# Mamba-2 and attention decoder step on one core: chunk work put ahead of weight conversions, and the step sizes' series moved to GpSimd

## The chip, the cores and the metric

The kernel runs on one core of a Trainium2 chip. The core has five engines: TensorE (PE, matmuls into the PSUM banks), VectorE (DVE), ScalarE (ACT), GpSimd (POOL) and SyncE (SP, which only issues DMAs here). They run on their own and meet at semaphores. The metric is the device time of one launch in microseconds, the median of several runs; lower is better.

## What is computed

One inference step of a two-layer decoder for 256 prompt tokens and 8 sample tokens (N = 264 columns, the model width is 1024). Everything is float32. Layer 0 is half-SwiGLU, Mamba-2 mixer, half-SwiGLU, gated per-layer embedding; layer 1 has sliding-window attention in the mixer's place. The part that the change touches most is the mixer:

```python
def mamba2_mixer(u, w_in, conv_w, conv_b, dt_bias, a_log, d_skip, norm_g, w_out, ssm0, conv0):
    z, xbc, dt_raw = jnp.split(u @ w_in, [D_INNER, D_INNER + CONV_DIM], axis=-1)
    conv = conv_b + sum(xbc_full[:, k:k + t_len] * conv_w[k] for k in range(CONV_W))
    xs, bm, cm = jnp.split(jax.nn.silu(conv), [D_INNER, D_INNER + SSM_GROUPS * D_STATE], axis=-1)
    dt = jax.nn.softplus(dt_raw + dt_bias)          # the step sizes, 32 heads
    a = -jnp.exp(a_log)
    y, h_last = ssd_scan(xs, dt, a, bm, cm, ssm0)   # chunks of 128 tokens, 8 groups of 4 heads
    gated = (y + d_skip[:, None] * xs) * jax.nn.silu(z)
    gg = gated.reshape(bsz, t_len, 8, 256)
    gg = gg * lax.rsqrt(jnp.mean(gg * gg, axis=-1, keepdims=True) + EPS)
    return (gg * norm_g) @ w_out, h_last, ...
```

The softplus is computed as max(t,0) + 2·artanh(q) with q = e/(2+e), e = exp(-|t|), and artanh(q) by its series in q², summed from the last term inwards. In each chunk the scan needs decays between positions (an exponential), the products inside the chunk, a sum over the chunk for the state, and for the second chunk what the first one's state adds.

## The kernel before

**Units.** Every weight matrix is cut into units of 128×1024. A unit is loaded by SyncE into one of four ring slots (`raw`); ScalarE rounds it to a high part (`whi`, L976) and VectorE subtracts to get the low part (`wlo`, L1388). These two are called the conversion here. TensorE then does 24 matmuls for a unit, three for each 128 rows (L435 to L437: high with high, high weights with low data, low weights with high data). In each engine's program `ahead(stage, i, s)` in slot `s` converts the unit that is four places further on, so that unit `s+4` is converted in slot `s`; ScalarE's half waits until TensorE has used unit `s`.

**The stage "sin".** It is the input projection of the mixer, 49 units in 49 slots, in an order written by hand (`SIN`): slot 0 is the step sizes' unit, slots 1 to 3 are `z` tiles, then come eight groups of four `conv` tiles, with further `z` tiles between them. For each slot every engine has its own list of what it does, in program order:
- TensorE: `sin_unit(s)`, then the small matmuls. A unit may only start when an older bank has been taken: unit 9 and later ones wait for the take of unit s-2.
- VectorE: the take (L1435, bank times `rstd`), three taps of the convolution for the previous slot's tile (L1636), `ahead`, and then whatever else stands in the slot.
- ScalarE: `ahead`, the convolution's last tap (`tap_last`, L1133), silu of the previous tile (L1139 or L1144), and whatever else stands in the slot. It loads a table when it changes between exponential, silu and root.
- GpSimd: a copy of each `conv` tile's tail (L2016), small products for the sample tokens, the sum of pairs of squares (L2046) and some DMAs.

**Step sizes.** VectorE takes the unit of slot 0 and starts (`dt_take`, `dt_start` in slot 1), runs the series in slots 2 and 3 (`dt_series`, L1604) and closes it (`dt_end`, L1617 to L1620). In slot 4 ScalarE's `gather_steps` makes eight copies into `dd` (L1186, L1187, tile `small`), and TensorE turns them in slot 7 (`pre_tokens`, L840). Ahead of its slots GpSimd prepares constants (L1994 to L2009, `pre_const`).

**Chunks.** For group g the slots C = `CHUNK_AT[g]` (14, 17, 21, 25, 30, 35, 41, 46), C+1 and C+2 hold: on TensorE `chunk_in` (L744 to L757: transposes and the decay's exponents, for chunk 0 in slot C, for chunk 1 in C+1) and `chunk_out` (L770, L775; chunk 0 in C+1, chunk 1 in C+2); on VectorE `chunk_in` (three operations that read the bank, L1710 to L1712), `decay` (L1732, it waits for ScalarE's exponential L1167), `carry` (L1719; L1723 to L1727) and in C+3 `finish`; on ScalarE `select` (L1158) and the exponential in `decay_exp`. TensorE's L744 for the next chunk waits for VectorE's L1712, its L770 for L1732, its L784 (`add_inter`) for L1723.

**Gate and sums.** In the slots `GATE_AT` VectorE multiplies by the silu of z (`gate`, L1752), ScalarE squares two tiles (L1230), GpSimd adds the two (L2046), and one slot later TensorE sums over the partitions (`norm_sums`, L822). After the eighth group come a root and a reciprocal, and then the output projection.

**Attention.** Eight pairs of heads go through scores (L561 to L565), maxima, exponentials (L1305), probabilities, `transposes` (L575), and `weighted_sum` (L589 to L593), with the rotary products `turn` (L547, L548). VectorE's `low_o(t)` (L1906) empties the bank that `weighted_sum(t+1)` writes.

## Time and profile before

| | before |
|---|---|
| median of 3 runs | 1243.44 us (1242.85 to 1243.95) |
| the profiled execution's own time | 1243.75 us |
| its span, from first to last instruction | 1241.9 us |
| mean granted TensorE clock | 0.994 of full speed |
| busy share of the span | TensorE 97%, VectorE 71%, ScalarE 56%, GpSimd 18% |
| stage "sin" | 211 to 445 us of the span |

The profile is of one execution. A busy share is an average over stages with different limits. The time outside the span, 1.85 us, belongs to the launch. Times in the text are microseconds from the start of the span.

### The profile page before, as it was taken

How to read it: one execution, taken by the hardware profiler on the slowest of the kernel's cores; microseconds unless marked ns; L12 is line 12 of the kernel's file. 1: busy time of each engine (PE TensorE's matmuls, PEld its weight loads, DVE VectorE, ACT ScalarE, POOL GpSimd, SP SyncE). 2: the span in 40 equal slices, each digit the busy share in tenths (PEclk: the TensorE clock that was granted, in tenths of full speed). 3: DMA queues.
4: the chain of work that ended last, by engine and by line, in shares of the span. 5: the costliest groups of instructions: out<-in, count | busy, mean ns of one | idle time of the engine just before them, and what ended most of it. 6: DMA issues, size and time to landing. Idle time of an engine off the chain costs nothing.

```text
span 1241.9 us, 26744 instructions
## 1 busy us (share of the span) xinstructions
PE 1207.8 (97%) x9887; PEld 1172.6 (94%) x9887; DVE 882.6 (71%) x1405; ACT 691.3 (56%) x1098; POOL 225.5 (18%) x332
## 2 busy tenths in 40 slices
PE   7999999889999999999999999999999999999998
PEld 7999999878888899999999989999998899999998
DVE  6667646978888876767744988788369758776447
ACT  6444436666566546555545774555357656445335
POOL 0000003212121110122244333332015310000001
PEclk9999999989999999999999999999999999999999
DMA  7665555645444445858786666766753146555552
GB/s 281 233 201 183 185 173 172 217 142 174 141 151 152 140 147 179 325 186 285 227 322 222 228 238 216 260 198 223 253 162 103 60 136 196 176 186 182 175 185 87
DMA packets 61424, 239.08 MB, mean 193 GB/s; under 512 B 7080, under 2 KB 8272, under 8 KB 56976
## 3 DMA queue, kind: packets, MB, share of 16 engines
q1 hardware_dynamic: 55008, 197.01, 47.7%
q0 software_dynamic: 6064, 40.66, 9.3%
q8 instruction: 42, 0.69, 0.2%
q10 hardware_dynamic: 288, 0.54, 0.1%
q14 instruction: 22, 0.18, 0.0%
HBM read 226.87 MB, written 13.39 MB: 193 GB/s over the span
## 4 chain that ended last, share of the span: by engine, by line
PE 79%; DVE 12%; ACT 5%; issue 4%; DMA 0%; DVEq 0%; SPq 0%; POOL 0%; ACTq 0%
PE bank L435 24%; PE bank L436 24%; PE bank L437 24%; DVE wlo L1388 3%; ACT whi L976 2%; DVE xl L1407 1%; DVE xact L1636 1%; PE bank L467 1%; PE bank L775 1%; PE bank L770 1%; DVE x L1418 1%; DVE rstd L1429 1%; DVE gu L1435 1%; PE bank L811 0%; ACT L1167 0%
## 5 line engine op out<-in xcount | busy, mean ns | idle before, releaser
L1388 DVE TENSOR_TENSOR wlo<-raw,whi 128x1024 fp32r<-128x1024 f32 x369 | 458.6, 1247 | 259.2 <-ACT whi L976 258.1
L435 PE MATMUL bank<-xh,whi 128*128 128x264 f32 x2024 | 583.6, 288 | 14.7 <-DVE xl L1407 9.8
L436 PE MATMUL bank<-xl,whi 128*128 128x264 f32 x2024 | 575.7, 284 | 0.0
L437 PE MATMUL bank<-xh,wlo 128*128 128x264 f32 x2024 | 575.3, 284 | 0.0
L976 ACT ACTIVATE whi<-raw 128x1024 fp32r<-128x1024 f32 x369 | 387.6, 1054 | 271.7 <-PE bank L437 262.4
L435 PEld LDWEIGHTS bank<-xh,whi 128*128 128x128 f32 x2024 | 383.4, 189 | 20.2 <-DVE wlo L1388 11.6
L436 PEld LDWEIGHTS bank<-xl,whi 128*128 128x128 f32 x2024 | 383.7, 190 | 0.9
L437 PEld LDWEIGHTS bank<-xh,wlo 128*128 128x128 f32 x2024 | 381.8, 189 | 0.0
L435 PE MATMUL bank<-hh,whi 128*128 (+1 forms) x896 | 255.9, 286 | 1.7 <-DVE xact L1503 0.9
L437 PE MATMUL bank<-hh,wlo 128*128 (+1 forms) x896 | 255.0, 285 | 0.0
L436 PE MATMUL bank<-hl,whi 128*128 (+1 forms) x896 | 254.4, 284 | 0.0
L435 PEld LDWEIGHTS bank<-hh,whi 128*128 128x128 f32 x896 | 168.6, 188 | 3.4 <-DVE xact L1503 1.1
L436 PEld LDWEIGHTS bank<-hl,whi 128*128 128x128 f32 x896 | 169.1, 189 | 0.1
L437 PEld LDWEIGHTS bank<-hh,wlo 128*128 128x128 f32 x896 | 168.6, 188 | 0.0
L1043 ACT ACTIVATE hh<-gu 128x264 fp32r<-128x264 f32 (+1 forms) x88 | 37.4, 425 | 164.0 <-DVE gu L1447 164.0
L1980 POOL TENSOR_TENSOR sq<-sq 128x264 f32<-128x264 f32 x42 | 34.0, 809 | 419.2 <-ACT sq L1014 414.8
L1435 DVE TENSOR_TENSOR gu<-bank,rstd 128x264 f32<-128x264 f32 x192 | 82.1, 429 | 19.2 <-PE bank L437 17.0
L1452 DVE TENSOR_TENSOR hl<-gu,hh 128x264 f32 (+1 forms) x88 | 42.4, 482 | 28.9 <-ACT hh L1043 28.9
L2115 POOL TENSOR_TENSOR xact<-xact,da_bc 128x512 f32<-128x512 f32 x32 | 38.9, 1217 | 101.8 <-PE bank L437 101.8
L1636 DVE SCALAR_TENSOR_TENSOR xact<-under,vs,xact 128x256 f32<-128x256 f32 x96 | 46.6, 485 | 3.2 <-ACT xact L1133 0.9
L1447 DVE TENSOR_TENSOR gu<-gu 128x264 f32<-128x264 f32 x88 | 44.9, 510 | 0.1
L2120 POOL TENSOR_TENSOR xact<-xact 128x512 f32<-128x512 f32 x20 | 29.6, 1481 | 60.6 <-PE bank L437 60.6
(309 smaller groups left out, 1002.9 us busy)
## 6 DMA issues: line engine op xcount, KB each, us to landing
raw<-weights SPq DMA_DIRECT2D x369, 512.0 KB, 3.5
under<-ssm POOLq DMA_DIRECT2D x8, 1024.0 KB, 5.1
xact<-ssm POOLq DMA_DIRECT2D x8, 1024.0 KB, 7.3
out_ssm_s<-xact POOLq DMA_DIRECT2D x8, 1024.0 KB, 5.3
xact<-dtx_rows POOLq DMA_DIRECT2D x5, 1024.0 KB, 11.0
zs<-dtx_rows POOLq DMA_DIRECT2D x2, 1024.0 KB, 13.6
x<-xT SPq DMA_DIRECT2D x2, 528.0 KB, 5.5
xact<-stat_rows POOLq DMA_DIRECT2D x2, 528.0 KB, 6.5
```

What stands on the lines that cost most here:

```text
L435: pe.matmul(out, whi[:, w, c], rh, start=start, stop=False)
L436: pe.matmul(out, whi[:, w, c], rl, start=False, stop=False)
L437: return pe.matmul(out, wlo[:, w, c], rh, start=False, stop=stop)
L976: act.activation(whi[:, s, :], raw[:, s, :], ACT.Copy).then_inc(hi_ready, 1)
L1043: act.activation(dst, gu[:, 2 * p + 1, :], ACT.Copy).then_inc(hh_ready, 1)
L1388: dve.tensor_tensor(wlo[:, s, :], raw[:, s, :], whi[:, s, :].bitcast(F32), ALU.subtract).then_inc(lo_ready, 1)
L1435: dve.tensor_tensor(dst, src[:, 0:N], rstd[:, :], ALU.mult).then_inc(a_free, 1)
L1447: dve.tensor_tensor(gu[:, 2 * p + 1, :], gu[:, 2 * p, :], gu[:, 2 * p + 1, :], ALU.mult).then_inc(h_ready, 1)
L1452: dve.tensor_tensor(one(hl), gu[:, 2 * p + 1, :], one(hh).bitcast(F32), ALU.subtract).then_inc(hl_ready, 1)
L1636: dve.scalar_tensor_tensor(out=out, in0=xr[:, k:k + T], scalar=vs[:, V_CW + CT * k + c:V_CW + CT * k + c + 1], in1=out, op0=ALU.mult, op1= ...
L1980: pool.tensor_tensor(sq3[:, 0, :], sq3[:, 0, :], sq3[:, m, :], ALU.add).then_inc(sq_pair, 1)
L2115: pool.tensor_tensor(by_head(part), by_head(part), da_bc[:, 2 * k:2 * k + 2, 4 * q:4 * q + 4].unsqueeze(3).to_broadcast([P, 2, 4, 64]), AL ...
```

## The change

On VectorE the chunk work, the carries and the gate of a slot now stand in front of the slot's conversion (`ahead`) in all slots that hold chunk work, with the gate behind the carries; the first chunk's part is moved one slot forward, to slot 13. On ScalarE the first exponential of a group stands ahead of the gate's square, the very first one right behind the exponentials of slot 12, and `gather_steps` stands behind `tap_last`. The series has one term less and runs on GpSimd, which also makes half of the eight copies. The last group's two squares are summed by TensorE without GpSimd. In attention `transposes(4)` goes ahead of `turn(7)`, and `low_o(3)` ahead of a conversion.

```diff
-DT_STEPS = 18
+DT_STEPS = 9
@@ TensorE
             def norm_sums(g):
-                pe.wait_ge(gated_pair, g + 1)
+                if g < G - 1:
+                    pe.wait_ge(gated_pair, g + 1)
+                else:
+                    pe.wait_ge(gated_sq, G)
...
-                pe.matmul(rows, ones[:, 0:32], gsq[:, 0, :], start=True, stop=True).then_inc(gated_sum, 1)
+                tiles = 1 if g < G - 1 else 2
+                for k in range(tiles):
+                    mm = pe.matmul(rows, ones[:, 0:32], gsq[:, k, :], start=k == 0, stop=k == tiles - 1)
+                mm.then_inc(gated_sum, 1)
             def pre_tokens():
                 pe.wait_ge(dt_a_step, 3)
+                pe.wait_ge(dt_ready, 2)
@@ TensorE, attention
             scores(5)
+            transposes(4)
             turn(7)
-            transposes(4)
@@ ScalarE
             def gather_steps():
-                act.wait_ge(dt_d_step, DT_STEPS)
+                act.wait_ge(dt_ready, 1)
                 for q in range(4):
-                    act.activation(dd[0:32, c], xact[r, 8, 0:66], ACT.Copy)
                     ins = act.activation(dd[32:64, c], xact[r, 14, 0:66], ACT.Copy)
@@ ScalarE, slots
+                if kind == "conv":
+                    tap_last(s_, i)
                 if s_ == 4:
                     gather_steps()
-                if kind == "conv":
-                    tap_last(s_, i)
...
                     ins.then_inc(pre_a, 1)
+                    decay_exp(0)
+                if s_ in CHUNK_AT[1:]:
+                    decay_exp(2 * CHUNK_AT.index(s_))
                 if s_ in GATE_AT:
...
-                if s_ in CHUNK_AT:
-                    decay_exp(2 * CHUNK_AT.index(s_))
@@ VectorE
-                dt_step(dve.tensor_scalar(a_, s2_, 1.0 / 17, None, ALU.mult))
+                dt_step(dve.tensor_scalar(a_, s2_, 1.0 / 15, None, ALU.mult))
+                dt_step(dve.tensor_scalar(avec[:, :], avec[:, :], -1.0, None, ALU.mult))
@@ VectorE, slots
-                if 0 < s_ < len(SIN):
-                    ahead("sin", 0, s_)
                 if s_ == 1:
                     dt_start()
-                if s_ == 2:
-                    dt_series((15, 13, 11, 9))
-                if s_ == 3:
-                    dt_series((7, 5, 3))
-                    dt_end()
+                chunks = s_ == CHUNK_AT[0] - 1 or s_ in CHUNK_AT[1:] or s_ - 1 in CHUNK_AT or s_ - 2 in CHUNK_AT
+                if 0 < s_ < len(SIN) and not chunks:
+                    ahead("sin", 0, s_)
...
-                if s_ in GATE_AT:
-                    gate(GATE_AT.index(s_))
...
-                    if s_ == CHUNK_AT[g]:
+                    if s_ == (CHUNK_AT[g] if g > 0 else CHUNK_AT[0] - 1):
                         chunk_in(2 * g)
                         decay(2 * g)
...
+                if s_ in GATE_AT:
+                    gate(GATE_AT.index(s_))
+                if s_ < len(SIN) and chunks:
+                    ahead("sin", 0, s_)
@@ VectorE, attention
             maxima(5)
+            low_o(3)
             ahead("q", 0, 7)
             rope_sin(7)
             rope_add(7)
-            low_o(3)
@@ GpSimd, behind the constants
+            t_, q_, m_, s2_, a_ = (xact[:, 8 + k, 0:66] for k in (0, 4, 2, 5, 6))
+            pool.wait_ge(dt_d_step, DT_STEPS)
+            for k in (13, 11, 9, 7, 5, 3):
+                link(pool, pool_step, steps, pool.tensor_scalar(a_, a_, 1.0 / k, None, ALU.add))
+                link(pool, pool_step, steps, pool.tensor_tensor(a_, a_, s2_, ALU.mult))
+            link(pool, pool_step, steps, pool.tensor_scalar(a_, a_, 1.0, 2.0, ALU.add, ALU.mult))
+            link(pool, pool_step, steps, pool.tensor_tensor(a_, a_, q_, ALU.mult))
+            pool.tensor_tensor(a_, a_, m_, ALU.add).then_inc(dt_ready, 1)
+            pool.wait_ge(dt_ready, 1)
+            link(pool, pool_step, steps, pool.tensor_scalar(t_, a_, avec[:, :], None, ALU.mult))
+            for q in range(4):
+                r, c = slice(32 * q, 32 * q + 32), slice(66 * q, 66 * q + 66)
+                ins = pool.tensor_copy(dd[0:32, c], xact[r, 8, 0:66])
+                link(pool, pool_step, steps, ins) if q < 3 else ins.then_inc(dt_ready, 1)
+            pool.wait_ge(dt_ready, 2)
@@ GpSimd, slots
-                if s_ in NORM_AT:
+                if s_ in NORM_AT[:G - 1]:
                     pair_squares(NORM_AT.index(s_))
```

`link` lets the engine wait for the operation that it has just issued.

## Rows read from the trace of the kernel before

**Rows 1.** The page, busy time of each engine in the span.

```profile
PE 1207.8 (97%) x9887; PEld 1172.6 (94%) x9887; DVE 882.6 (71%) x1405; ACT 691.3 (56%) x1098; POOL 225.5 (18%) x332
```

**Rows 2.** TensorE's waits, 205 to 445 us: total, times, longest.

```profile
PE bank L744 <- DVE sq L1712: 4.9, 3, 4.2
PE bank L770 <- DVE sq L1732: 3.2, 5, 1.3
PE bank L435 <- DVE under L1435: 2.8, 1, 2.8
...
PE bank L822 <- POOL gsq L2046: 0.7, 1, 0.7
PE bank L784 <- DVE under L1723: 0.7, 1, 0.7
```

**Rows 3.** Windows: busy time and instructions of each engine, granted clock, DMA.

```profile
100.00:200.00 100.00, 100.00 (x826) 100.00 (x825) 54.44 (x66) 41.49 (x50) 0.00 (x0) 1.00 0.56 179
...
237.90:241.30 3.40, 3.40 (x18) 3.40 (x17) 3.33 (x6) 1.77 (x4) 0.67 (x2) 0.50 0.81 272
...
265.20:272.00 6.80, 5.88 (x25) 4.72 (x26) 5.15 (x11) 5.50 (x9) 1.13 (x1) 0.50 0.49 162
```

**Rows 4.** Timeline of VectorE, step sizes: start, us, instruction, idle before.

```profile
218.97 1.38 DVE L1388 TENSOR_TENSOR wlo<-raw,whi 128x1024 fp32r<-128x1024 f32 x1
...
223.43 1.01 DVE L1604 SCALAR_TENSOR_TENSOR xact<-xact 128x66 f32<-128x66 f32 x4
...
230.53 1.53 DVE L1636 SCALAR_TENSOR_TENSOR xact<-under,vs,xact 128x256 f32<-128x256 f32 x3 [0.89 <-ACT xact L1133]
231.97 1.22 DVE L1388 TENSOR_TENSOR wlo<-raw,whi 128x1024 fp32r<-128x1024 f32 x1
...
236.03 0.42 DVE L1435 TENSOR_TENSOR under<-bank,rstd 128x264 f32<-128x264 f32 x1
```

**Rows 5.** Timeline of GpSimd, 211 to 262 us.

```profile
213.29 0.63 POOL L1995 TENSOR_TENSOR gu<-gu,vs 128x256 f32<-128x256 f32 x1
214.00 0.63 POOL L1997 TENSOR_TENSOR gu<-zs,vs 128x256 f32<-128x256 f32 x1
...
228.31 1.04 POOL L2016 COPY tailraw<-under 128x11 f32<-128x11 f32 x1 [6.75 <-DVE under L1435]
229.71 0.19 POOL L2016 COPY tailraw<-under 128x11 f32<-128x11 f32 x1 [0.35 <-DVE under L1435]
233.60 0.39 POOL L2016 COPY tailraw<-under 128x11 f32<-128x11 f32 x1 [3.70 <-DVE under L1435]
```

**Rows 6.** Timeline of ScalarE, 225 to 235 us.

```profile
227.74 0.26 ACT L1186 ACTIVATE small<-xact 32x66 f32<-32x66 f32 x1 [3.95 <-DVE xact L1620]
```

**Rows 7.** Timeline of VectorE, first chunk.

```profile
260.68 1.23 DVE L1388 TENSOR_TENSOR wlo<-raw,whi 128x1024 fp32r<-128x1024 f32 x1 [1.62 <-ACT whi L976]
...
264.98 0.42 DVE L1710 COPY under<-bank 128x256 f32<-128x256 f32 x1
```

**Rows 8.** Timeline of ScalarE, first chunk.

```profile
259.30 0.26 ACT L1223 ACTIVATE dt_d<-bank 64x128 f32<-64x128 f32 x1
...
264.57 1.28 ACT L1167 ACT_TABLE_LOAD   x1
```

**Rows 9.** Timeline of TensorE, first chunk.

```profile
266.12 0.80 PE L744 MATMUL bank<-xact 128*128 128x128 f32 x2 [4.19 <-DVE sq L1712]
...
275.15 0.33 PE L770 MATMUL bank<-sq 128*64 128x128 f32 x2
```

**Rows 10.** VectorE's waits, 205 to 445 us.

```profile
DVE sq L1732 <- ACT sq L1167: 7.2, 7, 1.9
```

**Rows 11.** Timelines of GpSimd and TensorE, sum of the first group.

```profile
294.99 0.76 POOL L2046 TENSOR_TENSOR gsq<-gsq 128x264 f32<-128x264 f32 x1 [5.99 <-ACT gsq L1230]
...
296.32 0.63 PE L822 MATMUL bank<-gsq,cs 128*32 128x264 f32 x2
```

**Rows 12.** Timeline of TensorE, attention.

```profile
975.35 0.44 PE L589 MATMUL bank<-under,xact 128*64 128x128 f32 x4 [1.01 <-DVE hl L1906]
```

More of the change, by code:

```diff
@@ L239, in trunk_kernel @@
         dt_d_step = sem("dt_d_step")
+        dt_ready = sem("dt_ready")
         dt_a_step = sem("dt_a_step")
@@ L1599, in dt_take @@
                 dt_step(dve.tensor_scalar(m_, t_, 0.0, None, ALU.max))
-            def dt_series(ks):
-                for k in ks:
-                    dt_step(dve.scalar_tensor_tensor(out=a_, in0=a_, scalar=1.0 / k, in1=s2_, op0=ALU.add, op1=ALU.mult))
             def dt_start():
@@ L1612, in dt_start @@
                 dt_step(dve.tensor_tensor(s2_, q_, q_, ALU.mult))
-                dt_step(dve.tensor_scalar(a_, s2_, 1.0 / 17, None, ALU.mult))
-            def dt_end():
-                dt_step(dve.scalar_tensor_tensor(out=a_, in0=a_, scalar=1.0, in1=q_, op0=ALU.add, op1=ALU.mult))
-                dt_step(dve.scalar_tensor_tensor(out=a_, in0=a_, scalar=2.0, in1=m_, op0=ALU.mult, op1=ALU.add))
-                link(dve, dve_step, steps, dve.tensor_scalar(avec[:, :], avec[:, :], -1.0, None, ALU.mult))
-                dt_step(dve.tensor_scalar(t_, a_, avec[:, :], None, ALU.mult))
+                dt_step(dve.tensor_scalar(a_, s2_, 1.0 / 15, None, ALU.mult))
+                dt_step(dve.tensor_scalar(avec[:, :], avec[:, :], -1.0, None, ALU.mult))
                 assert n_dt[0] == DT_STEPS
```

## The prediction

> **What bounds the kernel now.** I read the page first, then the waits, the windows and the timelines of the one stage that the edits touch. TensorE is busy for 97% of the span [rows 1], so only the holes in its row can be won. The stage "sin" (the units of the mixer's input projection with the chunked state sums between them) runs from 211 to 445 us of the span. TensorE's waits there add up to 12.9 us, and they name their releasers [rows 2]: one wait of 2.8 us on a take (L1435, the copy of a finished bank to SBUF), 4.9 us on the end of `chunk_in` (L1712), of which 4.2 is one wait, 3.2 us in five waits on `decay` (L1732), and 0.7 us each at L784 and L822. Both long waits are followed by a stretch in which the granted clock is at its lower level, 1.2 GHz [rows 3]. In the first, 3.4 us long, 18 matmuls are issued; at full clock 826 are issued in 100 us, 0.121 us apart, so that 18 need 2.2 us: 1.2 us lost. In the second, 6.8 us, I estimate 2.4 us lost. The two sites therefore cost 2.8+1.2 and 4.2+2.4 us, 10.6 together; that is what the change plays for.
>
> **Site 1: the step sizes.** Before, seven series steps (four of them 1.01 us), two closing ones, a negation and a product (0.9 us) stand between VectorE's conversions [rows 4], and at the first `conv` slot ScalarE waits 3.9 us for them, makes eight copies of 0.27 us, and only then does its `tap_last` (L1133) [rows 6]. VectorE's taps, 0.89 us late for that, start at 230.53 [rows 4], its conversion for unit 9 ends at 231.97+1.22 = 233.20, and the take of unit 7, which TensorE's unit 9 waits for, comes at 236.03; TensorE restarts at 236.60.
>
> After, VectorE is rid of ten small operations (0.25 us each, 2.5 us) and the series is 20 GpSimd operations: six pairs, three closing ones, the product, four copies. Each waits for the one before. A free GpSimd chain of 256 elements goes from start to start in 0.71 us (213.29 to 214.00, 0.63 of it the operation), an 11 element copy takes 0.19 [rows 5]; in between, 66 elements take 0.32 and 0.40 with the link. The 15 operations up to `dt_ready` 1 would then need 6.0 us. But a copy that needs 0.19 took 1.04 under a conversion of VectorE, and 0.39 between two taps: it came out when VectorE's operation ended [rows 5]. So I lay the chain against VectorE's schedule. `dt_start` (now with the negation, 1.9 us) stands ahead of the conversion for unit 5; it ends at about 221.0, and GpSimd's constants end about then too. From there VectorE runs take and conversion in turn (1.65 us), and I count two GpSimd operations for each pair, one held by the conversion and one started in the take: eight operations by 227.6. Three taps let one through each (229.2). Then four more in 1.6 us, because VectorE has stopped: operation 15 ends at 230.8.
>
> VectorE stops because ScalarE now stands in `gather_steps` until `dt_ready` 1. Behind it are a z silu (0.3), the conversions for unit 9 and all later taps. ScalarE: 230.8+0.1+4×0.27+0.3+1.05 = 233.3, VectorE's half 1.25 more: unit 9 is converted at 234.6, against 233.20. VectorE works without a pause in this stretch, so all behind it is 1.4 later: the take of unit 7 at 237.5, unit 9 at 238.0. TensorE also loses 0.9 at unit 5 (its conversion ends at 222.3, where it ended at 218.97+1.38 = 220.35) and 1.7 at `pre_tokens`, which waits for GpSimd's copies (232.8). These two lie before the wait for unit 9 and only shorten it. If the shorter holes leave the clock full, the 1.4 us are paid back by the 1.2 us of the low clock: site 1 is worth 0. Below: a chain that is held once by each of seven VectorE operations and needs 0.83 us elsewhere (the price of 256 elements) ends near 235.7: 5 us lost. Above: a chain that nothing holds ends at 227.0, and all 4.0 us are won. I take 0, as the held copies are the nearest rows.
>
> The Trainium skill (GPSIMD Engine Reference, Performance versus the Vector engine) speaks against the move: a two-input operation takes about twice VectorE's time. With VectorE's 0.23 us for 66 elements the operations would take 0.46, and site 1 would be 1 to 2 us worse than by my interpolation; no GpSimd operation of this size is in the trace.
>
> **Site 2: the first chunk.** TensorE stood at L744 until 266.12, since VectorE did `chunk_in(0)` at 264.98 to 266.06: behind a conversion for which it had waited 1.62 us, taps and another conversion. ScalarE was late for that conversion because of its exponentials with a table load of 1.28, and it loaded the table again at 264.57 [rows 7, 8]. After, chunk 0 follows the taps of slot 13: VectorE 259.1+0.2 (`pre_decode`), `chunk_in` to 260.4; ScalarE goes on from 259.30+0.26 = 259.56 with select 0.39 and the exponential 0.60 without a load, and `decay(0)` ends at 261.3. TensorE arrives at L744 at 266.12-4.19 = 261.9: no wait. What is late next is chunk 1. ScalarE's conversions of slots 13 and 14 are 1 us later, it must load the silu table, wait for VectorE's last tap (264.8), convert (266.5), do the taps of slot 15 after its take (266.6), select, load and exponential: 269.5. TensorE's `decode_rows(0)` waits for that exponential; it is reached at 267.5 and ends at 270.7, where `chunk_out(1)` starts, against 275.15 [rows 9]: 4.5 us won of 6.6.
>
> This is not kept whole. The gate now stands behind the carries and ahead of the conversion. VectorE loses its cover for the wait on ScalarE's exponential (idle 0.4 to 1.9 us before `decay`, 7.2 us in seven waits [rows 10]): before, the conversion filled part of it, and its 1.2 us now come after. Two such delays put `gate(0)` at 291.2 to 291.9; the square ends at 292.6, GpSimd's pair sum (0.76) is held by the conversion that now follows the gate, and TensorE's sum L822 starts at 293.7, against 296.32 [rows 11]. So 2.6 us of the 4.5 are left, and TensorE has a new wait there.
>
> **The other chunks.** TensorE's 3.2 us on `decay`, 0.7 at L744 (without the long one) and 0.7 at L784. L744 goes, since `chunk_in` is 1.2 us earlier. The first `decay` of a group waits for ScalarE, not for VectorE, and gains nothing except in slots 30 and 46, where the exponential now stands ahead of the square (0.65): 1.3 and 0.7 us are won there. The second `decay` comes 1 us earlier, but the sum L822 behind it later. L784 goes: its carry stood behind conversion and gate. At L822 the last pair sum (0.75) goes, a second matmul pair (0.45) comes: 0.3. Sum of what can be won 3.9; with bounds of 0 (every wait replaced) and 4.5 I take 2.5. A conversion that is 3 us later costs nothing itself: four units of 2.9 us lie between it and its use.
>
> **Attention.** TensorE waits 1.0 us for `low_o(3)`, until 975.35 [rows 12]. Moved ahead of a conversion (1.2) and three small rope operations it ends 2 us earlier, and the transposes of pair 4 no longer stand behind 1 us of `turn(7)`: 0.8 won, between 0 (the exponentials were last) and 1.5.
>
> **Sum.** 0 + 2.6 + 2.5 + 0.8 = 5.9 us off the profiled execution's 1243.75 (1241.9 of it span) is 1237.85; the median of the runs is 0.3 below that execution, so 1237.5.
>
> **Rivals.** (a) The series hides: TensorE never waits for GpSimd, and site 2 keeps all. 4.0+6.6+3.9+0.8 = 15.3: 1228.1. For it: the stretches in which GpSimd was idle (6.7 us after 221.57); against: ScalarE's queue. (b) Slower: the chain on GpSimd is late, and all conversions wait behind `gather_steps`. Each us by which operation 15 ends after 229.4 costs one us. It eats the other gains from 235.4 on, 0.97 us per operation, and from 238 the kernel is over 0.2% slower: 1246. Here a GpSimd operation that has started must also hold VectorE. The rows show that only as 1.38 for a conversion instead of 1.21 [rows 4]. The Trainium skill (SBUF — State Buffer, SBUF: two separate sides) calls the shared port pair an exclusive lock for the whole instruction in both directions. By that, the 11 operations up to VectorE's halt would put up to 11×0.32 = 3.5 us on VectorE as well; the 0.17 of the row does not bear that out. (c) The waits only change their names: `decay` still ends last on ScalarE's exponential, L822 waits for the gate, site 1 is lost by 1.5: 1241 to 1245, say 1243.
>
> **Chances.** Forecast (gains of 3 to 10 us) 0.60; (a) 0.12; (b) 0.12; (c) 0.16. The forecast's own range is 1233.5 to 1240.5. The range with no more than 2 in 10 left out reaches from 1231, between forecast and (a), to 1243.5, into (b) and (c). A measurement here can tell about 0.2%, 2.5 us. Faster: 0.56+0.12+0.04 = 0.72; same: 0.04+0.04+0.10 = 0.18; slower 0.10.
>
> **What would show it.** Site 1: ScalarE's wait ahead of its first copy to `small`, now released by GpSimd; conversion 9 near 234.6; GpSimd operations of 0.3 us where VectorE rests and longer where it converts. Site 2: L744 without a wait, TensorE waiting about 2 us for the second exponential, no low clock near 265. Later: L822 waiting for POOL, L784 gone. Wrong it would be if operation 15 ended well before 229 or after 233, or if the low clock came back behind new holes (1 to 2.5 us each).

## The result, and the profile after

The changed kernel takes 1245.96 us (median of 20 runs, 1244.64 to 1248.15), the kernel before 1244.07 (20 runs, 1242.55 to 1245.7). The ratio is 1.0015, with a 95% interval of 1.0009 to 1.0021: 1.9 us slower, where 6 us faster was forecast. That lies inside the 0.2% taken as no change, and outside the forecast range. One execution of all that follow (in experiment 2) took 1305.03 us at a mean granted clock of 0.85; it is in no median and no ratio here.

The profiled execution took 1247.58 us (span 1245.7), 1.6 above its median, so part of its 3.8 us over the span of before isn't the change's. Its mean granted clock is 0.993; 15 of the 20 runs have 0.994 or more. Where the time arises can be read by setting the same events side by side. First the lines of TensorE's waits from 205 to 445 us, as in [rows 2]:

```profile
PE bank L828 <- POOL gsq L2057: 5.6, 7, 1.4
PE bank L848 <- POOL small L2020: 2.3, 1, 2.3
PE bank L797 <- ACT sq L1175: 2.3, 1, 2.3
PE bank L436 <- DVE under L1443: 1.8, 1, 1.8
PE bank L436 <- DVE wlo L1396: 1.4, 2, 0.8
PE bank L771 <- DVE sq L1729: 1.1, 2, 0.6
```

The waits at L744, L784 and most of those at L770 are gone (the lines are L745, L785 and L771 now), as the change intended. In their place stand seven waits at L828, the squares' sum (L822 before), and one at L848, the transposes of the step sizes. The total is 14.5 us, against 12.9 in [rows 2].

The same events of TensorE in its timeline, first of the kernel after:

```profile
265.45 0.38 PE L745 MATMUL bank<-xact 128*128 128x128 f32 x2
...
272.99 1.07 PE L797 MATMUL bank<-under,dact 128*32 128x256 f32 x16 [2.25 <-ACT sq L1175]
273.99 0.33 PE L771 MATMUL bank<-sq 128*64 128x128 f32 x2
...
295.86 0.63 PE L828 MATMUL bank<-gsq,cs 128*32 128x264 f32 x2 [0.63 <-POOL gsq L2057]
...
426.77 0.63 PE L828 MATMUL bank<-gsq,cs 128*32 128x264 f32 x2 [0.88 <-POOL gsq L2057]
...
441.93 1.08 PE L828 MATMUL bank<-gsq,cs 128*32 128x264 f32 x4
...
719.41 0.59 PE L436 MATMUL bank<-xh,whi 128*128 128x264 f32 x1 [1.20 <-DVE xl L1415]
```

and three of before that [rows 9, 11] don't hold:

```profile
427.07 0.63 PE L822 MATMUL bank<-gsq,cs 128*32 128x264 f32 x2
...
440.80 0.63 PE L822 MATMUL bank<-gsq,cs 128*32 128x264 f32 x2 [0.71 <-POOL gsq L2046]
...
717.34 0.39 PE L435 MATMUL bank<-xh,whi 128*128 128x264 f32 x1 [1.20 <-DVE xl L1407]
```

| event | before | after | lag |
|---|---|---|---|
| GpSimd's constants [rows 5] | 213.29 | 214.64 | +1.35 |
| take of unit 7 [rows 4] | 236.03 | 239.72 | +3.69 |
| L744, first chunk [rows 9] | 266.12 | 265.45 | -0.67 |
| L770, second chunk [rows 9] | 275.15 | 273.99 | -1.16 |
| sum of group 0 [rows 11] | 296.32 | 295.86 | -0.46 |
| sum of the sixth group | 427.07 | 426.77 | -0.30 |
| last sum | 440.80 | 441.93 | +1.13 |
| second hole of a unit at 717 | 717.34 | 719.41 | +2.07 |
| end of the span | 1241.9 | 1245.7 | +3.8 |

The first 1.35 us arise ahead of everything that was changed and the comparison starts from there. The step sizes lose 2.3 us, the first chunk wins 4.9, the first sum takes 0.7 back, and the groups between 296 and 427 us win nothing. Up to the last sum 1.4 are then lost, and they are a stretch at the lower clock (below): TensorE's L814 at 428.25 is 0.30 ahead of its row of before (L813, 428.55), and 24 matmuls later L771 at 433.09 is 1.23 behind (L770, 431.86), with no wait between. Another 1.0 is there by 491 (the next row that both have starts at 491.38 for 489.25): the last sum has four matmuls and holds the next unit for 1.00 us instead of 0.56, and 0.3 is a wait for a conversion. The order alone (experiment 1) loses the same 1.0 there, so it belongs to the change. Behind 717 two stretches at the lower clock take 1.4 and 1.5 us (719 us, and the second half of the one at 982), and attention wins 1.1 between them.

The granted clock in the profile's windows of the kernel after (columns as in [rows 3]):

```profile
241.20:244.60 3.40, 3.40 (x18) 3.40 (x17) 3.33 (x7) 1.38 (x3) 1.05 (x2) 0.50 0.74 246
428.90:432.30 3.40, 3.40 (x18) 3.40 (x17) 2.90 (x5) 2.13 (x3) 0.00 (x0) 0.51 0.08 12
719.10:722.50 3.40, 3.09 (x14) 3.09 (x15) 2.77 (x5) 3.38 (x5) 1.40 (x2) 0.50 0.19 39
981.90:988.70 6.80, 6.80 (x49) 5.93 (x50) 2.39 (x10) 2.61 (x10) 3.52 (x8) 0.50 0.06 20
```

The stretch at 1.2 GHz near 265 is gone. The one behind unit 9 has stayed, and a new one stands at 429, behind the 0.88 us wait at L828. Another stands at 719, behind holes of 0.96 and 1.20 us that the kernel before has too (its row 717.34); in the kernel before the granted clock is 1.00 in the whole window from 715 to 721. The one at 982 is there before the change as well, but half as long (3.4 us).

### The step sizes

GpSimd's timeline of the kernel after, and under it VectorE's and ScalarE's:

```profile
222.66 1.37 POOL L2011 TENSOR_SCALAR xact<-xact 128x66 f32<-128x66 f32 x1 [0.66 <-DVE avec L1617]
224.12 1.31 POOL L2012 TENSOR_TENSOR xact<-xact 128x66 f32<-128x66 f32 x1
225.51 1.44 POOL L2011 TENSOR_SCALAR xact<-xact 128x66 f32<-128x66 f32 x1
227.03 1.34 POOL L2012 TENSOR_TENSOR xact<-xact 128x66 f32<-128x66 f32 x1
228.46 0.38 POOL L2011 TENSOR_SCALAR xact<-xact 128x66 f32<-128x66 f32 x1
...
232.82 0.32 POOL L2015 TENSOR_TENSOR xact<-xact 128x66 f32<-128x66 f32 x1
```

```profile
222.54 1.23 DVE L1396 TENSOR_TENSOR wlo<-raw,whi 128x1024 fp32r<-128x1024 f32 x1
223.68 0.42 DVE L1443 TENSOR_TENSOR zs<-bank,rstd 128x264 f32<-128x264 f32 x1
224.02 1.21 DVE L1396 TENSOR_TENSOR wlo<-raw,whi 128x1024 fp32r<-128x1024 f32 x1
...
235.67 1.23 DVE L1396 TENSOR_TENSOR wlo<-raw,whi 128x1024 fp32r<-128x1024 f32 x1 [5.62 <-ACT whi L984]
```

```profile
233.18 1.06 ACT L1194 ACTIVATE small<-xact 32x66 f32<-32x66 f32 x4 [5.49 <-POOL xact L2015]
```

The first four operations of the series come out when a conversion of VectorE ends (223.77, and the next ones), and each has missed the gap behind it: the conversion is over at 223.77, GpSimd's operation at 224.03, the next conversion starts at 224.02, GpSimd's next operation at 224.12. So one operation passes in 1.45 us. Where VectorE makes taps or rests, the other eleven take 4.7 us, 0.43 each; four of them start inside the three taps (228.45 to 230.05) and take 0.33 to 0.44, so no hold shows there. Meanwhile ScalarE stands for 5.5 us and VectorE for 5.6.

### A sum of squares

Group 0 in the kernel after, VectorE, ScalarE and GpSimd:

```profile
292.25 0.42 DVE L1720 TENSOR_TENSOR under<-bank,tok 128x256 f32<-128x256 f32 x1
...
293.37 0.70 DVE L1749 TENSOR_TENSOR zs<-zs,xact 128x528 f32<-128x528 f32 x1
293.99 1.22 DVE L1396 TENSOR_TENSOR wlo<-raw,whi 128x1024 fp32r<-128x1024 f32 x1
```

```profile
294.10 0.65 ACT L1240 ACTIVATE gsq<-zs 128x528 f32<-128x528 f32 x1 [0.84 <-DVE zs L1749]
```

```profile
294.83 0.98 POOL L2057 TENSOR_TENSOR gsq<-gsq 128x264 f32<-128x264 f32 x1 [6.84 <-ACT gsq L1240]
```

The gate (L1749) stands behind the three operations of the carry, the square behind the gate, the pair sum behind the square and under a conversion (0.98 us for 0.76 in [rows 11]), and TensorE, which has the sum in its program one slot behind the gate, waits for it until 295.86. Six other groups do the same.

### The profile page after: what moved, and what is told of

Its sections match the earlier page's. It is cut to its first block, busy times and chain, and to the rows that moved or that the text cites. A ratio compares the mean times of both kernels' runs of the same rounds, so it can differ in the third digit from the quotient of the medians.

```text
span 1245.7 us, 26753 instructions
## 1 busy us (share of the span) xinstructions
PE 1209.1 (97%) x9889; PEld 1174.3 (94%) x9889; DVE 879.6 (71%) x1395; ACT 688.8 (55%) x1094; POOL 234.1 (19%) x351
## 4 chain that ended last, share of the span: by engine, by line
PE 75%; DVE 13%; ACT 6%; issue 4%; POOL 1%; DMA 1%; DVEq 0%; SPq 0%; ACTq 0%; POOLq 0%
PE bank L436 23%; PE bank L437 23%; PE bank L438 23%; DVE wlo L1396 4%; ACT whi L984 2%; DVE xact L1633 1%; DVE xl L1415 1%; PE bank L468 1%; ACT L1175 1%; DVE x L1426 1%; DVE rstd L1437 1%; DVE gu L1443 1%; DMA x<-xT 1%; DMA xact<-stat_rows 1%; POOL gsq L2057 0%
```

## The experiments

All ratios are to the kernel before, measured in turn with it on the same chip, with 95% intervals; microseconds won or lost are worked out from the ratio and its 1244. A lag is the start of an event less the start of the same event in the kernel before.

**1. The change in three parts.** The first has only the hunks of the series and the copies, the second only those of the order, the early first chunk, the exponentials and the last sum, the third only the two moves in attention. Together they are the changed kernel.

The series alone:

> The kernel before with one part of the change alone: the step sizes' series and half of the copies on GpSimd. Theory (what the trace of the changed kernel shows): four operations of the series are each held to the end of a VectorE conversion, the last value comes at about 231.8 us instead of the forecast 230.8, unit 9 starts 2.3 us later than before, the low clock stays: 2.0 to 2.5 us slower than before. Rival (the forecast): 0, the shorter holes leave the clock full. Second rival: the loss of the first stretch is made up by the wait of the first chunk (4.2 us, it is VectorE's), which then would shrink only if VectorE weren't late as well: under 1 us slower.

1246.15 us, 1.0021 (1.0011 to 1.0030): 2.6 us slower. The forecast of 0 falls. Its TensorE waits 2.6 us at the transposes, 0.3 at unit 9 and 1.4 in two smaller ones; the stretch at 1.2 GHz follows the transposes here.

The order alone:

> The kernel before with the chunk work, carries and gate in front of the conversions on VectorE, the exponentials in front of the squares on ScalarE, and the last group's sum on TensorE; series and attention as before. Theory: the first chunk's wait and its low clock go (3.5 to 4.5 us won), the other chunks win nothing, as each wait for a decay or a carry comes back as a wait for the pair sum on GpSimd (0.6 to 1.3 us at each of seven sums), and the end of the stage loses 1 to 2 us: 1 to 3 us faster than before. Rival (the forecast): 5.1 us faster. Rival: no gain at all, if the low clock of the first chunk comes back at a later hole.

1242.07 us, 0.9992 (0.9983 to 1.0001): 1.0 us faster, where the prediction had 5.1, at the lower end of the 1 to 3 of the text above. Its waits in TensorE:

```profile
PE bank L827 <- POOL gsq L2056: 5.4, 7, 1.4
PE bank L435 <- DVE under L1442: 2.9, 1, 2.9
PE bank L796 <- ACT sq L1173: 2.3, 1, 2.3
```

The seven waits at the sums are there without the series on GpSimd. The first and the last sum:

```profile
293.54 0.63 PE L827 MATMUL bank<-gsq,cs 128*32 128x264 f32 x2 [0.39 <-POOL gsq L2056]
...
438.08 1.08 PE L827 MATMUL bank<-gsq,cs 128*32 128x264 f32 x4
```

Against 296.32 and 440.80 before, the lag is -2.78 at the first sum and -2.72 at the last, and -1.71 at 489: from the first sum on the order wins nothing and then loses the 1.0 us named above. There is no stretch at 1.2 GHz at 429 in this execution, though the wait ahead of there is nearly the same (0.90 us at the sixth sum for 0.88).

Attention alone:

> The kernel before with only the two moves in attention. Forecast: 0.8 us faster (0 to 1.5). Theory from the changed kernel's trace: the weighted sum of pair 4 starts 1.1 us earlier there, but a stretch at the lower clock behind it is twice as long (6.8 us for 3.4) and takes 1 to 1.8 us: 0 to 0.5 us slower. If that stretch has nothing to do with the moves, 0.8 to 1.1 faster.

1242.83 us, 0.9994 (0.9982 to 1.0006): 0.7 us faster, as the prediction had it (0.8), though the interval reaches from 2.2 faster to 0.7 slower and so holds the 0 to 0.5 slower of the text above too. The three parts add up to 0.9 us slower, each with about 1.1 us either way; the whole change measured 1.9.

**2. Two cures for the sums.** Both start from the order alone. One leaves the gate where it was ahead of the change's move, in front of the chunk work:

```diff
+                if s_ in GATE_AT:
+                    gate(GATE_AT.index(s_))
                 for g in range(G):
                     if s_ == CHUNK_AT[g] + 3:
                         finish(g)
...
-                if s_ in GATE_AT:
-                    gate(GATE_AT.index(s_))
                 if s_ < len(SIN) and chunks:
```

> As the run with the order of the chunk work alone, but the gate stands ahead of the chunk work and the carries, as in the kernel before. Theory: the 5.4 us at TensorE's seven sums come from the gate behind the decays and carries and from GpSimd's pair sum held by the conversion behind it; with the gate first the square is done before it: these waits fall to 1 to 2 us, 0.5 to 1 us come back at decays and carries (0.7 us of gate ahead of them): 2.5 to 4 us faster than with the order alone. Rival: ScalarE's square stands behind its exponential and is as late as before, then nothing changes.

1237.21 us, 0.9944 (0.9931 to 0.9957): 7.0 us faster than before, 6.0 faster than the order alone, more than the 2.5 to 4 expected. TensorE's waits:

```profile
PE bank L435 <- DVE under L1442: 2.9, 1, 2.9
PE bank L796 <- ACT sq L1173: 2.3, 1, 2.3
PE bank L770 <- DVE sq L1739: 1.1, 2, 0.6
PE bank L827 <- ACT gsq L1239: 0.8, 1, 0.8
```

5.4 us in seven waits have become 0.8 in one; those at the decays (L770) are what they were with the order alone, so the gate in front of them costs nothing there. A wait of 0.7 us at L744 for a silu (`ACT xact L1145`) is new. So the waits give 3.9 of the 6.0 us; the rest I can't assign (the two intervals together allow about 2 either way). The first and the last sum:

```profile
292.05 0.63 PE L827 MATMUL bank<-gsq,cs 128*32 128x264 f32 x2
...
433.25 1.08 PE L827 MATMUL bank<-gsq,cs 128*32 128x264 f32 x4 [0.82 <-ACT gsq L1239]
```

The lag goes from -4.27 to -7.55: with the gate first the same order wins 3.3 us between the two sums, 2.1 of them left at 489. In the first group VectorE and GpSimd:

```profile
288.89 0.70 DVE L1759 TENSOR_TENSOR zs<-zs,xact 128x528 f32<-128x528 f32 x1
...
290.63 1.73 DVE L1395 TENSOR_TENSOR wlo<-raw,whi 128x1024 fp32r<-128x1024 f32 x1
```

```profile
290.52 0.75 POOL L2056 TENSOR_TENSOR gsq<-gsq 128x264 f32<-128x264 f32 x1 [5.91 <-ACT gsq L1239]
```

The pair sum is finished at 291.27, before TensorE comes to its sum at 292.05.

The other cure leaves the gate behind the carries and asks for the sum later:

```diff
-NORM_AT = [t_ + 1 for t_ in GATE_AT]
+NORM_AT = [t_ + (2 if g_ in (0, 1, 2, 3, 4, 5) else 1) for g_, t_ in enumerate(GATE_AT)]
```

> As the run with the order of the chunk work alone, but TensorE's and GpSimd's part of the first six groups' sums one slot later. Theory: the waits at the first six sums (about 5 us) are there because the sum comes one slot behind a gate that now stands behind the carries; a slot later (2.9 us) they have gone: 3 to 5 us faster than the run with the order alone. Rival: the waits only move on, to the next decay, as ScalarE's exponential and the conversions set the pace: within 1 us of it.

1238.28 us, 0.9955 (0.9941 to 0.9968): 5.6 us faster than before, 4.6 faster than the order alone. The waits for the pair sum fall to 0.4 us; the decays have 0.5 for 1.1, so nothing moved on to them. A wait of 0.9 us at one sum has no releaser in the profile.

**3. How much of it is GpSimd's.** TensorE sums both tiles of every group, and GpSimd adds none; the gate stays behind the carries.

```diff
-                if g < G - 1:
-                    pe.wait_ge(gated_pair, g + 1)
-                else:
-                    pe.wait_ge(gated_sq, G)
+                pe.wait_ge(gated_sq, g + 1)
...
-                tiles = 1 if g < G - 1 else 2
+                tiles = 2
...
-                if s_ in NORM_AT[:G - 1]:
-                    pair_squares(NORM_AT.index(s_))
```

> As the run with the order of the chunk work alone (gate behind the carries), but TensorE sums both tiles in all groups, GpSimd adds no pair. It splits the 5.4 us at the sums: the pair sum takes 0.98 us under a conversion and the second pair of matmuls costs 0.25 to 0.45. If GpSimd's hold is most of it, 4 to 5 us faster than with the order alone; if it is the late gate and square, 1 to 3 us, and TensorE's waits at L827 name ScalarE's square.

1240.73 us, 0.9977 (0.9966 to 0.9987): 2.9 us faster than before, 1.9 faster than the order alone. That is the size expected if the late gate is most of it. But the waits left are 0.6 us in two, for ScalarE's square, so the two shares can't be told apart cleanly: taking GpSimd out ends nearly all the waits, and most of what it wins is spent on the second pair of matmuls in seven groups (an estimate: 7 times the 0.44 of the last sum, 3.1 us).

**4. The gate's place in the changed kernel itself.** The gate's diff of experiment 2, applied to the changed kernel, with nothing else changed.

> The changed kernel with one line moved: the gate stands ahead of finish, chunk work and carries. Theory: the gate's place alone took 5 to 6 us (the run with the order alone against the one with the gate first: 6.0): 5 to 6.5 us faster than the changed kernel, 3 to 4.5 faster than the kernel before, although the series stays on GpSimd. Rival: with the series on GpSimd VectorE is 2.3 us behind and the gate's place matters less: 2 to 3 us.

1240.39 us, 0.9964 (0.9951 to 0.9976). The changed kernel stands at 1.0015, so the place of one call was worth 6.3 us, as expected, and without that move the change would have been 4.5 us faster than before, inside the forecast range. The waits at the step sizes are still there (2.6 us at L848).

**5. The first chunk by itself.** On the kernel before, with the exponential right behind those of slot 12; all else as it was.

```diff
-                if 0 < s_ < len(SIN):
+                if 0 < s_ < len(SIN) and s_ != CHUNK_AT[0] - 1:
                     ahead("sin", 0, s_)
...
-                    if s_ == CHUNK_AT[g]:
+                    if s_ == (CHUNK_AT[g] if g > 0 else CHUNK_AT[0] - 1):
                         chunk_in(2 * g)
                         decay(2 * g)
...
+                if s_ == CHUNK_AT[0] - 1:
+                    ahead("sin", 0, s_)
```

> The kernel before with only the first chunk's part a slot earlier, ahead of the conversion of slot 13, and its exponential right behind those of slot 12. Forecast for this part: 4.5 us won, of which 2.6 are kept where the gate stands behind the carries. Theory: with the gate in its old place nothing takes it back: 3.5 to 5.5 us faster than before, more than the whole order alone (1 to 2.2). Rival: the second chunk then waits for its decay, which stands behind a conversion again, and half is lost at once: 1.5 to 3.

1241.58 us, 0.9982 (0.9972 to 0.9992): 2.2 us faster, under the range that I gave and in that of the rival. But its mechanism isn't what happened:

```profile
261.70 0.38 PE L744 MATMUL bank<-xact 128*128 128x128 f32 x2
...
269.24 1.07 PE L796 MATMUL bank<-under,dact 128*32 128x256 f32 x16 [2.26 <-ACT sq L1167]
```

TensorE waits for the second exponential, as forecast, and wins all the same: the lag is -4.91 here (274.15 before), -4.92 at the first sum (291.40) and -4.88 at the last (435.92). With the gate in its old place nothing is taken back. The profiled execution is only 4.0 us shorter (span 1237.9 for 1241.9), since it has a stretch at 1.2 GHz at 712.5, far behind the change:

```profile
712.50:715.90 3.40, 3.40 (x16) 3.40 (x17) 2.77 (x4) 3.38 (x5) 1.40 (x2) 0.51 0.27 41
```

The twelve runs spread from 1238.38 to 1244.89, and the median lies 2 us above the trace. The clock is part of that: the three slowest runs (1244.10 to 1244.89) have a mean granted clock of 0.992, the other nine 0.995 to 0.997. But those nine still spread from 1238.38 to 1242.73, so the rest is open.

**6. The step sizes: whose waiting is it?** Three kernels have only the series and copies of the change, each with one thing different. In the first, ScalarE makes its copies a slot later:

```diff
-                if s_ == 4:
+                if s_ == 5:
                     gather_steps()
```

> As the run with the series and half of the copies on GpSimd alone, but ScalarE makes its copies a slot later, behind the conversion for unit 9 and the last tap of slot 5. Theory: what delayed unit 9 was ScalarE standing in front of its copies, with the conversion queued behind; without it unit 9 starts without a long wait, TensorE's 2.6 us at the transposes of the step sizes stay: 1.5 to 2.5 us faster than that run, about as the kernel before. Rival: the delay is GpSimd's hold on VectorE or VectorE's own work; then unit 9 is as late as before and nothing changes.

1246.89 us, 1.0021 (1.0013 to 1.0030): nothing gained; my theory, that ScalarE's queue delayed unit 9 and so set the loss, falls. The wait at unit 9 is gone, but with the series alone it was only 0.3 us, and the one wait for GpSimd's copies has grown from 2.6 to 3.4:

```profile
PE bank L842 <- POOL small L2010: 3.4, 1, 3.4
PE bank L436 <- DVE wlo L1389: 1.4, 2, 0.8
```

In the second, TensorE's transposes are a slot later too (`if s_ == PRE_AT + 1: pre_tokens()` in its list):

> As the run before (copies of ScalarE a slot later) with TensorE's transposes of the step sizes one slot later too. Theory: the 2.6 us at the transposes are only GpSimd's chain of 20 operations ending at 234; a slot later it has ended, neither hole is left and the clock stays full: 3.5 to 5 us faster than the run with the series on GpSimd alone, 1.5 to 3 faster than the kernel before. Rival: the work of VectorE behind it (its copies out of the bank, pre_sums) is then late, and TensorE waits in slots 9 to 12: no better than the run before.

1244.97 us, 1.0010 (1.0001 to 1.0019): 1.4 us better, not the 3.5 to 5 expected. The transposes wait 0.5 us, and then unit 9 waits, for a take behind a conversion of VectorE that stood behind ScalarE's copies:

```profile
235.23 0.24 PE L842 MATMUL bank<-cs,small 64*128 64x64 f32 x1 [0.54 <-POOL small L2010]
237.56 0.56 PE L436 MATMUL bank<-xh,whi 128*128 128x264 f32 x1 [2.02 <-DVE under L1436]
```

Both readers of the series wait for the same end. Moving TensorE's reader as well takes its wait away, but then the conversions that stand behind ScalarE's copies are what TensorE waits for.

In the third the end itself is moved: four of the six pairs are left out of the series (the terms 13, 11, 9 and 5), eight operations of twenty.

```diff
-            for k in (13, 11, 9, 7, 5, 3):
+            for k in (7, 3):
```

> As the run with the series and half of the copies on GpSimd alone, but GpSimd's chain has only two of the six pairs (the terms 13, 11, 9 and 5 are left out): 12 operations for 20, 7 for 15 up to ScalarE's copies. It tells whether the length of the dependent chain is what costs. Theory: the first four operations are held to the end of four VectorE conversions, as in that run, the other eight that fall away needed 0.46 us each: ScalarE's copies and TensorE's transposes 3.7 us earlier, neither hole of 2.6 us at the transposes nor a late unit 9; 3 to 4 us faster than that run, 0.5 to 2 faster than the kernel before. Rival: GpSimd's place behind its constants or the two waits that hand over between the engines are what costs: less than 1 us better than that run.

1242.82 us, 0.9996 (0.9987 to 1.0005): 3.1 us faster than with the whole chain, as the theory said. The first four operations are held as before (1.31 to 1.44 us), and the last one ahead of ScalarE's copies starts 7.05 us after the first one's 221.07, for 10.16 in the changed kernel (232.82 less 222.66): 3.1 us there too. TensorE doesn't wait for GpSimd at all (its row at L842 has no wait):

```profile
221.07 1.37 POOL L2001 TENSOR_SCALAR xact<-xact 128x66 f32<-128x66 f32 x1 [0.66 <-DVE avec L1610]
...
228.12 0.45 POOL L2005 TENSOR_TENSOR xact<-xact 128x66 f32<-128x66 f32 x1
...
231.14 0.28 PE L842 MATMUL bank<-cs,small 64*128 64x64 f32 x1
```

It still waits 1.1 us at unit 9, and no stretch at 1.2 GHz follows in this execution. So the length of the dependent chain sets the loss.

**7. A cheaper form of the same idea.** The series stays on VectorE, a term shorter; four copies go to GpSimd, and ScalarE's last tap goes ahead of its copies.

```diff
-                    act.activation(dd[0:32, c], xact[r, 8, 0:66], ACT.Copy)
...
-                if s_ == 4:
-                    gather_steps()
                 if kind == "conv":
                     tap_last(s_, i)
+                if s_ == 4:
+                    gather_steps()
...
-                    dt_series((15, 13, 11, 9))
+                    dt_series((13, 11, 9))
...
+            pool.wait_ge(dt_d_step, DT_STEPS)
+            for q in range(4):
+                r, c = slice(32 * q, 32 * q + 32), slice(66 * q, 66 * q + 66)
+                ins = pool.tensor_copy(dd[0:32, c], xact[r, 8, 0:66])
+            ins.then_inc(dt_ready, 1)
```

> The kernel before with the step sizes' series left on VectorE (a term shorter), four of the eight copies on GpSimd, and ScalarE's copies behind its last tap. Theory: VectorE is rid of one operation (0.25 us) and of the 0.89 us for which its taps waited for ScalarE's eight copies, so unit 9 starts about 1.1 us earlier, 1.7 us of hole instead of 2.8, with or without the lower clock behind it (1.2 us): 1 to 2.3 us faster than before, and 3 to 4.5 faster than with the series on GpSimd. Rival: GpSimd's four copies are held by VectorE's conversions and TensorE waits for them at the transposes of slot 7 as long as it is early: no change.

1243.03 us, 0.9991 (0.9982 to 0.9999): 1.1 us faster, the lower end of the forecast. TensorE's wait at unit 9 falls from 2.8 [rows 2] to 2.0 us, and the lower clock behind it stays.

**8. Together.** The order with the gate first, attention, and the kernel of 7:

> What the runs so far point to, put together: chunk work and carries in front of the conversions with the gate ahead of them, the last sum on TensorE, the two moves in attention, the series on VectorE a term shorter with four copies on GpSimd and ScalarE's last tap ahead of its own. If the parts add up: 7.0 + 1.1 + 0.7 = 8.8 us faster than the kernel before, 8 to 9.5. Rival: the gains meet in the same holes (the wait for the second exponential takes what the step sizes give), then 7 to 7.5.

1236.45 us, 0.9935 (0.9922 to 0.9948): 8.1 us faster than before, so the parts add up nearly whole. Its profiled execution, the fastest of five, took 1233.64 us at a mean granted clock of 0.999; the other four have 0.995 to 0.997. With the first six sums a slot later as well:

> The best version so far (gate first, series on VectorE, four copies on GpSimd, attention's two moves) with the first six sums one slot later as well. Two cures for one wait: TensorE's waits at these sums are nearly gone already (0.8 us in one), so within 1 us of the best version. If it is 1 to 3 us faster, the gate's early place had itself taken something from the decays.

1234.88 us, 0.9936 (0.9923 to 0.9950): by the ratios no difference, as expected. The gate's place and the sums' slot are two cures for one wait.

## Why the prediction was wrong

5.9 us were forecast to be won, 1.9 were lost. Measured by themselves, the order gave 1.0 of 5.1 (4.1 short), the series -2.6 instead of 0, attention 0.7 of 0.8; the remaining 1.0 lies within the intervals.

**The other chunks: +2.5 forecast.** This is the step that failed. With the order alone the trace has -1.1 in its place (lag -2.78 at the first sum, -1.71 at 489), in the changed kernel -2.6, 1.5 of it in the stretch at the lower clock at 429. The gains are there: 3.2 us at L770 have become 1.1, and L744 and L784 are gone. The loss on the other side was named ("the sum L822 behind it later") and not priced, except for the first group. I had followed the chain gate, square, pair sum, TensorE's sum once, for group 0, and found TensorE waiting there; the same order stands in six more groups, and 5.6 us of waits came of it. The waits of these chunks went from 5.3 us (0.7, 3.2, 0.7 and 0.7) to 6.7 (5.6 and 1.1). The range I gave for this term, 0 to 4.5, allowed only for waits that are replaced one for one. With the gate first the trace has +2.1 for the same term, and the order gives 7.0 us in all; with the gate behind the carries it gives 1.0. (The gains that the prediction lists for this term add up to 3.7, not to its 3.9.)

**The first chunk: 4.5 won, 2.6 kept.** Right in what is won: L744 has no wait, TensorE waits 2.25 us for the second exponential (forecast about 2), and the second chunk gains 4.85 us against the step sizes' lag, 4.9 in experiment 5. What is given back was priced too high: 0.7 us instead of 1.9 in the changed kernel, 0.5 with the order alone. That the order alone keeps 2.8 at the first sum, close to the forecast 2.6, is luck: a stretch at 1.2 GHz behind the second exponential takes the 1.5 us that the late gate does not. In the changed kernel there is no such stretch near 265, with the order alone there is (270 to 273).

**Site 1: 0 forecast, 2.3 lost in the trace, 2.6 by itself.** The term was mis-sized, inside its bounds of -5 and +4, in two of its steps. First, "two GpSimd operations for each pair, one held by the conversion and one started in the take": it was one, since a held operation ends when the take is nearly over. The three taps, which were to let one through each, held nothing: four operations started inside them. In other places the price of 0.40 us with the link was about right (0.43). With GpSimd's start 0.3 us later than I had it, operation 15 ends at 233.14, less the 1.35 of the start 231.8, not 230.8; unit 9 starts at 240.29, less 1.35 238.9, not 238.0. Rival (b)'s rule, a microsecond for each one by which operation 15 ends after 229.4, gives 2.4 us for 231.8, and the trace shows 2.3. Second, the shorter holes did not leave the clock full: 2.26 and 1.84 us were followed by the lower clock as one of 2.8 had been, and the 1.2 us that were to pay for the delay stayed lost. (By the rows at 429 such a stretch costs 1.5 us, not 1.2: the 18 matmuls counted in its window include those that reach over its ends.) But the length of the holes was no ground to expect either: see the last section. The Trainium skill (GPSIMD Engine Reference, Performance versus the Vector engine), weighed against this move with "1 to 2 us worse", was nearer than my value, though not by its reason: two-input operations that nothing held took 0.32 to 0.38 us where VectorE's take 0.23 in the kernel before, 1.4 to 1.7 times and not twice, and the count of held ones made the rest.

**Attention: 0.8.** By itself 0.7, with an interval that also holds nothing. In the changed kernel's trace the weighted sum of pair 4 wins 1.1 us (the lag is +3.02 at the scores ahead, 972.67 for 969.65, and +1.89 at the sum, 977.24 for 975.35), and the stretch at 1.2 GHz behind it, 6.8 us instead of 3.4, takes 1.5 again. That was not in the forecast. The stretch near 980 is 6.8 us long in the profiled executions of four of the five kernels with the two moves, and 3.4 in all eleven without them.

**The rivals.** (b) named the late chain and its price rightly; it reached 231.8 of the 238 at which it would have decided alone. (c), "the waits only change their names", is nearest: it named L822 waiting for the gate. It had a chance of 0.16 and a time of 1243, since I let it eat the gains and not go below them. None of the rivals had the low clock behind the new waits, as at 429; the prediction names it only among its signs of being wrong, and the order alone shows that it need not come.

## What to carry to other kernels

When an operation is moved behind others, follow its result through every engine to its last reader, and price that wait in each repetition, not in one; then move the reader or leave the producer first. A chain of small dependent operations on GpSimd passed here at one operation for each conversion where VectorE converted without a pause (1.45 us each), and at 0.43 us each elsewhere: lay the chain against VectorE's rows before pricing it, and compare with the 0.25 us that each one costs on VectorE. Judge such a move by all readers of its end, since freeing one only hands the wait to the next.

## What the runs showed of the hardware

The hold between GpSimd and VectorE goes both ways. A 66 element operation of GpSimd takes 1.31 to 1.44 us when it meets a conversion, and 0.25 to 0.48 otherwise; and a conversion that started 0.11 us behind GpSimd's pair sum took 1.73 us instead of 1.22, that is, it lost about what the pair sum still had to run (0.64). The Trainium skill (SBUF — State Buffer, SBUF: two separate sides) says that whichever starts first gets the shared ports for its whole instruction, and that VectorE takes part with operations that have two inputs in SBUF. Both rows agree; the taps, which also read two tiles of SBUF (0.5 us each), show no hold. In the prediction I had read its lesser share (0.17 us) from a single row.

The lower clock doesn't follow from a hole alone, nor from its length. Behind the hole of 2.8 or 2.9 us at unit 9 a stretch of 3.4 us at 1.2 GHz stands in the profiled executions of the kernel before, the later sums, and experiments 3 and 5, and none in those of the order alone, attention alone and the gate first (granted clock 1.00 from 233 to 243 us). Behind the same two holes of 0.96 and 1.20 us near 717 some have such a stretch (the changed kernel, and those of experiments 3, 4 and 5) and others, the kernel before among them, have none. I didn't find what decides it. With matmuls 0.22 us apart instead of 0.121, each such stretch costs about 1.5 us, as much as many an edit here. So the profiles of two kernels can differ by several us through the clock alone; the ratios over many runs are what the comparisons above rest on.
